# One decoder layer on one core: the expert gather and its turn become one matmul group, and the front weights come laid out by the host

## The reference

```python
proj = h @ w_in                                # front weights: w_ada (modulation), w_in, w_o
x = x + g1 * (o @ w_o)
h = rms_norm(x, norm2_g) * (1.0 + sc2) + sh2
logits = h @ router_w + router_b
top_val, top_idx = lax.top_k(logits, 4)        # 4 of 32 experts for each token
gate = softmax(top_val)
# each expert e, for the tokens that picked it:
u = x_e @ w_up[e] + b_up[e]                    # w_up[e] 1024 x 2048
glu, lin = split(u)
act = min(glu, 7) * sigmoid(1.702 * glu) * (clip(lin, -7, 7) + 1)
y_e = act @ w_down[e] + b_down[e]              # w_down[e] 1024 x 1024
y[token] += gate * y_e
```

## Time and profile before

| | |
|---|---|
| times of three runs | 1163.48, 1164.04, 1168.39 us (median 1164.04) |
| time of the profiled execution | 1164.73 us |
| span of the profiled execution | 1163.0 us |
| PE busy (matmul) | 1115.0 us, 96%, 5666 records |
| PE loads (PEld) | 498.6 us, 43% |
| DVE, ACT, POOL busy | 411.7 us, 191.1 us, 28.7 us |
| moved by DMA | 460.96 MB, mean 396 GB/s over the span |

### The profile page before, as it was taken

How to read it: one execution, slowest core, us unless ns; L and a number is a source line. 1 busy time by engine, 2 the same in 40 slices (tenths; PEclk the granted TensorE clock), 3 DMA queues, 4 the chain that set the end, 5 groups by cost and what they waited for, 6 DMA issues and landing times.

```text
span 1163.0 us, 14304 instructions
## 1 busy us (share of the span) xinstructions
PE 1115.0 (96%) x5666; PEld 498.6 (43%) x5666; DVE 411.7 (35%) x841; ACT 191.1 (16%) x385; POOL 28.7 (2%) x57
## 2 busy tenths in 40 slices
PE   7999999999999999999999998999999999999996
PEld 4777778843333333333333333333333333333332
DVE  3134653343333333333333334333333333333334
ACT  2152223321111111111111111111111111111112
POOL 0101110000000000000000000000000000000001
PEclk9999999999999999999999998999999999999998
DMA  9998996999999999999999999999999999999995
GB/s 335 377 297 227 322 349 229 371 359 392 419 419 422 427 425 429 427 429 428 429 428 428 429 427 429 427 429 426 428 428 427 429 429 429 427 429 427 428 427 212
DMA packets 52474, 460.96 MB, mean 396 GB/s; under 512 B 7156, under 2 KB 8128, under 8 KB 26152
## 3 DMA queue, kind: packets, MB, share of 16 engines
q1 hardware_dynamic: 46160, 449.66, 93.4%
q0 software_dynamic: 2752, 9.47, 3.5%
q10 hardware_dynamic: 3512, 1.14, 0.5%
HBM read 455.60 MB, written 4.65 MB: 396 GB/s over the span
## 4 chain that ended last, share of the span: by engine, by line
PE 75%; DMA 22%; SPq 1%; DVE 1%; ACT 1%; issue 0%; DVEq 0%; ACTq 0%
PE bank L1433 28%; DMA ring<-in_w_up 18%; PE bank L1488 15%; PE bank L1095 9%; PE bank L1474 5%; PE bank L1404 4%; DMA ring<-in_w_down 3%; PE bank L1316 2%; PE bank L1451 2%; PE bank L1040 1%; DMA ring<-in_w_ada 1%; PE bank L1413 1%; PE bank L1199 1%; PE bank L1462 1%; SPq L473 1%; PE bank L1176 1%
## 5 line engine op out<-in xcount | busy, mean ns | idle before, releaser
L1433 PE MATMUL bank<-ring,arena 128*64 128x512 f32 x2016 | 448.2, 595 | 21.5 <-DMA ring<-in_w_up 20.2
L1433 PEld LDWEIGHTS bank<-ring,arena 128*64 128x64 f32 x2016 | 139.8, 137 | 320.1 <-issue 277.7
L1488 PE MATMUL bank<-ring,arena 128*64 128x512 f32 x992 | 220.1, 595 | 1.3 <-DMA ring<-in_w_down 1.3
L1488 PEld LDWEIGHTS bank<-ring,arena 128*64 128x64 f32 x992 | 68.6, 137 | 131.3 <-issue 129.1
L1095 PE MATMUL bank<-arena,ring 128*128 128x264 f32 x448 | 105.4, 390 | 0.8 <-DVE arena L1695 0.8
L2043 DVE COPY arena<-bank 128x512 f32<-128x512 f32 x32 | 22.1, 692 | 199.2 <-PE bank L1433 199.2
L901 ACT ACTIVATE arena<-bank 128x512 f32<-128x512 f32 x32 | 19.1, 598 | 439.5 <-PE bank L1433 439.5
L1095 PEld LDWEIGHTS bank<-arena,ring 128*128 128x128 f32 x448 | 83.1, 190 | 17.9 <-issue 4.5
L2097 DVE TENSOR_TENSOR arena<-bank,arena 128x512 f32<-128x512 f32 x32 | 22.1, 692 | 189.1 <-PE bank L1488 189.1
L2092 DVE TENSOR_TENSOR arena<-arena,bank 128x512 f32<-128x512 f32 x128 | 79.2, 681 | 5.4 <-PE bank L1474 5.4
L1474 PE MATMUL bank<-arena,gpickT 64*128 64x512 f32 x248 | 78.7, 628 | 0.0
(11 more groups left out here) (335 smaller groups left out, 701.2 us busy)
## 6 DMA issues: line engine op xcount, KB each, us to landing
ring<-in_w_up SPq DMA_DIRECT2D x125, 2048.0 KB, 28.5
ring<-in_w_down SPq DMA_DIRECT2D x61, 2048.0 KB, 27.6
ring<-in_w_ada SPq DMA_DIRECT2D x16, 1024.0 KB, 15.6
ring<-in_w_in SPq DMA_DIRECT2D x14, 1024.0 KB, 14.7
ring<-in_w_ada SPq DMA_DIRECT2D x16, 512.0 KB, 11.9
ring<-in_w_o SPq DMA_DIRECT2D x4, 1024.0 KB, 19.0
arena<-in_w_up SPq DMA_DIRECT2D x5, 512.0 KB, 18.5
arena<-in_w_down SPq DMA_DIRECT2D x5, 512.0 KB, 12.1
```

The costliest lines, as they stand in the source:

```text
L1433: last = mm(bank[64 * half:64 * half + 64, b, :], xe[:, par, k % 4, k // 4, :], src[:, 512 * half:512 * half + 512], start=(k == 0), stop= ...
L1488: last = mm(bank[64 * half:64 * half + 64, b, :], acts[:, k, :], src[:, 512 * half:512 * half + 512], start=(k == 0), stop=(k == KT - 1))
```

## The change

Four things are changed.

1. Gather and turn are one group of matmuls. `h2tok` is now the stationary operand (128 tokens x 128 features, every second float of a row) and `pick` the moving one (64 columns). The result has the features in the partitions at once. There are 16 matmuls for an expert in place of 4 matmuls, a copy on ACT and 4 transposes. `take_gathered`, `turn`, the tile `xg` and the semaphore `gathered` are gone; DVE makes the next pick when `turned` has come.
2. ACT writes `h2tok` in four pieces of 512 floats in place of two of 1024, and the first gather begins with the first two. To this end PE's logits come ahead of the second row turn, and the samples' statistics behind the logits.
3. `w_ada`, `w_in` and `w_o` come from the host in blocks as the kernel loads them, 128 x 2048 with 8 KB of consecutive bytes for each partition. The 16 loads of half a megabyte for the first part of `w_ada` are 8 of one. A block of `w_o` now holds two column groups m for all k, so that it is used up after the second of them.
4. Expert 1 is gathered in the middle of the up matmuls of expert 0. The residual's transposes come behind these, and the residual's copies on ACT in the first turn of the loop. On DVE the first gates and the second pick come ahead of the counts for overflowing experts.

```diff
-            if kind == "out" and s == 3:
-                return "wo_psum", KT
+            if kind == "out":
+                return "wo_psum", 2 * s + 2
...
-                if kind == "ada" and c == 0:
-                    h, j = s // 4, s % 4
-                    for row in range(2):
-                        sp.dma_start(ring[:, slot, D * row:D * row + D].rearrange("p (e n) -> p e n", e=2),
...
+                src = {"ada": a["w_ada"], "in": a["w_in"]}[kind][c, s] if kind != "out" else a["w_o"][s]
+                sp.dma_start(ring[:, slot, :], src).then_inc(sem(f"slot{slot}"), 16)
...
+            def take_rows_of(i, j):
+                act.wait_ge(sem("h2tok_psum"), 2 * j + i + 1)
+                od.did(A(h2tok[:, i, 512 * j:512 * j + 512], bank[:, 4 + 2 * i + j, :], ACT.Copy, scale=rst[:, i:i + 1]),
+                       sem("h2tok_sb"))
...
-            def take_gathered(n):
-                act.wait_ge(sem("gathered"), n + 1)
-                act.activation(xg, bank[:, 6, :], ACT.Copy).then_inc(sem("xg_ready"), 1)
...
             def gather(n, first_blocks=True):
                 pe.wait_ge(sem("pick_ready"), n + 1 if first_blocks else n + 2)
-                if isinstance(n, int) and n == 0:
-                    pe.wait_ge(sem("h2tok_sb"), 2)
-                else:
+                if not (isinstance(n, int) and n == 0):
                     pe.wait_ge(sem("xe_ready"), n * XE)
-                for i in range(2):
-                    for half in range(2):
-                        last = mm(bank[64 * half:64 * half + 64, 6, :], pick[:, i, :], h2tok[:, i, 512 * half:512 * half + 512],
-                                  start=(i == 0), stop=(i == 1))
-                last.then_inc(sem("gathered"), 1)
-
-            def turn(n):
-                pe.wait_ge(sem("xg_ready"), n + 1)
-                for j in range(4):
-                    c0 = 2 * P * (j // 2) + j % 2
-                    last = tr(bank[:, 6, P * j:P * j + P], xg[:, c0:c0 + 2 * P - 1:2], ident[:, :])
+                for half in range(2):
+                    if isinstance(n, int) and n == 0:
+                        pe.wait_ge(sem("h2tok_sb"), 2 * half + 2)
+                    for j in range(4):
+                        c0 = 512 * half + 2 * P * (j // 2) + j % 2
+                        for i in range(2):
+                            last = mm(bank[:, 6, P * j + 64 * half:P * j + 64 * half + 64], h2tok[:, i, c0:c0 + 2 * P - 1:2],
+                                      pick[:, i, :], start=(i == 0), stop=(i == 1))
                 last.then_inc(sem("turned"), 1)
...
             gather(0)
             samples_routed()
-            turn(0)
             keep_going(4)
...
             up(0, 0, UP_FIRST, lo, ro, first=True)
+            gather(1)
+            up(0, UP_FIRST, UPS - 1, lo, ro)
+            up(0, UPS - 1, UPS, lo, ro)
...
             for n, n0, q in experts(pe):
-                gather(n + 1)
+                if n0 > 0:
+                    gather(n + 1)
                 back(n)
-                turn(n + 1)
```

More of the change, by code:

```diff
@@ L148, in is_plain @@
     kind, c, i = what
-    return not ((kind == "ada" and (i == 7 or (c == 0 and i == 3))) or (kind == "in" and i == 1) or (kind == "out" and i == 3))
+    return not ((kind == "ada" and (i == 7 or (c == 0 and i == 3))) or (kind == "in" and i == 1) or kind == "out")
 FRONT_USED = {}
@@ L175, in front_round @@
 def front_round(n):
-    return sum(1 + (FRONT[m][:2] == ("ada", 0)) for m in range(n + 1) if FRONT_SLOT[m] == FRONT_SLOT[n])
+    return sum(FRONT_SLOT[m] == FRONT_SLOT[n] for m in range(n + 1))
 FRONT_PLAIN = sum(_PLAIN)
@@ L921, in _, with take_residual @@
             od.did(A(gateE[:, :, :], gateE[:, :, :], ACT.Exp), sem("gate_exp"))
-            for i in range(2):
-                act.wait_ge(sem("x1tok_psum"), i + 1)
-                od.did(A(acc[i], wide(4 - 2 * i), ACT.Copy), sem("x1tok_sb"))
+            def take_residual():
+                for i in range(2):
+                    act.wait_ge(sem("x1tok_psum"), i + 1)
+                    od.did(A(acc[i], wide(4 + 2 * i), ACT.Copy), sem("x1tok_sb"))
             def take_sample_rows():
@@ L1309, in wo_part @@
             def wo_part(m, ks):
+                ld = FRONT_AT[("out", 0, m // 2)]
+                if m % 2 == 0:
+                    use_front(ld)
                 for k in ks:
-                    ld = FRONT_AT[("out", 0, k // 2)]
                     if m == 0 and k % 2 == 0:
-                        use_front(ld)
                         pe.wait_ge(sem("on_ready"), k // 2 + 1)
-                    last = mm(bank[:, WO_BANK[m % 3], 0:T], ring[:, FRONT_SLOT[ld], D * (k % 2) + P * m:D * (k % 2) + P * m + P],
+                    c0 = 2 * P * k + P * (m % 2)
+                    last = mm(bank[:, WO_BANK[m % 3], 0:T], ring[:, FRONT_SLOT[ld], c0:c0 + P],
                               oT[:, k, :], start=(k == 0), stop=(k == KT - 1))
-                    if m == KT - 1 and k % 2 == 1 and k < KT - 1:
-                        last.then_inc(sem("weights_used"), 1)
                 return last
@@ L1358, in _ @@
             row_stats(KT - 1).then_inc(sem("stat_psum"), 1)
-            turn_rows(1)
-            pe.wait_ge(sem("sq_ready"), KT + 1)
-            mm(bank[:, 2, 2 * P:2 * P + KT * TS], ones[:, :], tmpT[:, :, TP:T], start=True, stop=True)
             pe.wait_ge(sem("lt_sb"), 1)
@@ L1366, in _ @@
             last.then_inc(sem("logit_psum"), 1)
+            pe.wait_ge(sem("sq_ready"), KT + 1)
+            mm(bank[:, 3, 2 * P:2 * P + KT * TS], ones[:, :], tmpT[:, :, TP:T], start=True, stop=True
+               ).then_inc(sem("logit_psum"), 1)
+            turn_rows(1)
             for k in range(2, KT):
@@ L1585, in _ @@
             back(NE - 2)
-            turn(NE - 1)
             combine(NE - 3, SUM_BANKS, NE, NE - 2)
@@ L2228 @@
     for name in _INS:
-        x = np.ascontiguousarray(inputs[name])
+        of, lay = LAID_OUT.get(name, (name, np.asarray))
+        x = np.ascontiguousarray(lay(np.asarray(inputs[of])))
         arrays[f"in_{name}"] = x
```

102 lines of the change are left out of this document (50 added, 52 removed).

## The result

| | before | after |
|---|---|---|
| median of four runs each, on one chip | 1164.22 us | 1202.45 us (1199.36 to 1209.95) |
| ratio | | 1.0334, 95% interval 1.0307 to 1.0361: slower |
| time and span of the profiled execution | 1164.73 and 1163.0 us | 1203.83 and 1202.0 us |
| PE busy, PEld busy | 96%, 43% | 98%, 49% |
| DVE, ACT busy | 411.7, 191.1 us | 411.7, 172.0 us |

The change costs 38.2 us; the forecast was 1210 us, 46 more. The four runs after spread by 10.6 us, and this goes with the mean clock that PE was granted: 0.985 in the run of 1209.95, 0.993 in that of 1199.36. Time less (1 - clock) x span gives 1189 to 1192 for all four.

The account below looks back on a forecast made before the run. It took PE and the DMAs as close limits, with 21.5 us of PE time spare. Span: 1163.0 - 21.5 + 68.4 + 1.4 - 0.6 + 0.1 - 2.3 = 1208.5, time 1210 us; own range 1202 to 1220, 8 in 10 1190 to 1236.

Parts of the forecast that it names:

- rival A: Gather: the stride is free, 0.111 us a record, a turn grows by 1.83 us, total 1196 us; chance 0.17.
- 30 gathers in the loop: Loop, experts 2 to 31: each gather lengthens its turn by 2.28 us, +68.4 us in all.
- PE's waits for weights vanish: Loop: PE's turn becomes level with the DMAs' 29.4 us, so its 21.5 us of waits for weights go.
- start of the first gather: Ahead of expert 0: -2.3 us from the front and -0.6 from the wait for ACT's copies, -2.9 us.
- first gather to expert 0's up: First expert: gather 1.74 us becomes 4.00, the samples' spreading (0.41) and the turn (0.48) go; +1.4 us.
- expert 0's up to expert 1's: First expert: 20.66 us between the up matmuls of experts 0 and 1 becomes 20.72, +0.1 us.
- What bounds the kernel: Whole kernel: PE and DMAs lie close; PE has 21.5 us to give away, and work beyond lengthens the kernel one to one.
- The gather: Loop: 32 records at 0.125 us, 4.00 us instead of 2.25, 0.53 for the change of width moved ahead; turn +2.28 us.
- The turn: Loop: the four removed transposes (0.48 us) save nothing, since `combine`'s fourth matmul waits for DVE anyway.
- rival B: Loop: the removed turn pays after all if `combine`'s fourth matmul is freed earlier, 14.5 us less, 1196 us; chance 0.07.
- The front: Front weights: loading in one 8 KB piece per partition removes about PE's wait for `w_ada`; -2.3 us, between 0 and -4.5.
- The marks that I named: New profile: loads near 260 ns, turns of 29.4 us, hardly any weight waits, DMA share below 1, longer DVE hold, `w_ada` wait below 1 us.

Follow-up runs that it names:

- Experiment 7: The kernel before with six more matmuls on constants in each turn of the loop, behind `combine`; 1181.36 us, ratio 1.0148.
- experiment 8: The changed kernel, but ACT writes the token rows with even and odd features apart, so that the gather's stationary operand is contiguous; 1195.35 us, ratio 1.0250.
- experiment 5: The kernel before with one edit: DVE takes the next expert's tokens ahead of the first bias; 1163.55 us, ratio 0.9992.
- experiment 4: The changed kernel, but DVE takes the next expert's tokens ahead of the bias; 1169.99 us, ratio 1.0052.
- experiment 1: The kernel before with the merged gather alone, everything else left as it was; 1204.11 us, ratio 1.0346.
- experiment 6: The kernel before with three more matmuls on constants in each turn of the loop, behind `combine`; 1166.28 us, ratio 1.0011.
- experiment 2: The changed kernel with the old gather and turn put back, all other edits kept; 1164.32 us, ratio 1.0004.
- experiment 9: The changed kernel with four constant matmuls of 512 columns, two ahead of the wait for the ranks and two ahead of the first gather; 1202.57 us, ratio 1.0329.
- experiment 10: The changed kernel with tokens taken ahead of the bias, contiguous token rows, and one constant matmul at each of two places before the first gather; 1168.62 us, ratio 1.0048.
- experiment 3: The kernel before with the host's layout of the front weights and the new `w_o` blocks alone; 1166.25 us, ratio 1.0016.

## Why the prediction was nearly right, and where it was not

The sum was +45.5 us of span, and +39.0 were measured. That the two are so near is in part luck: the gather's term was 7.5 us too high and the returned waits 5.2 too small, and the clock's fall, which the forecast didn't have, adds 4.9 against them. Without it the kernel would stand near 1198 us, below the forecast's own range (1202 to 1220) and at rival A's 1196. Its terms, with what the two traces show. "Start" is that of the first piece of chain named.

| term | predicted | measured | from |
|---|---|---|---|
| 30 gathers in the loop | +68.4 | +60.9 | turns of 29.08 and 27.05 us (means 29.17 and 27.14) |
| PE's waits for weights vanish | -21.5 | -26.7 | what is left of the sum once the other rows are taken, see below |
| start of the first gather | -2.9 | -1.4 | 236.88 to 235.50 |
| first gather to expert 0's up | +1.4 | +1.1 | 5.81 us at full clock against 4.70 |
| clock at the first gather | 0 | +4.9 | 9.77 - 5.81, and 7.96 - 7.02 in the first half of up |
| expert 0's up to expert 1's | +0.1 | +0.2 | 267.02 - 245.27 - 0.94 against 20.59 |

**What bounds the kernel: right, and it decided.** The loss follows the turn only beyond PE's spare time. Its size was a fifth too small. The list of waits shows 21.5 us, but a turn at the DMAs' pace takes 29.36 against 27.05 undisturbed, 2.3 us more. Its two waits in the timeline of PE before are only 0.52 and 1.24:

```profile
955.95 3.65 PE L1433 MATMUL bank<-ring,arena 128*64 128x512 f32 x16 [0.52 <-DMA ring<-in_w_up]
960.85 3.65 PE L1433 MATMUL bank<-ring,arena 128*64 128x512 f32 x16 [1.24 <-DMA ring<-in_w_up]
```

About 0.5 us of each such turn is lost and isn't in the list. 23 waits are about 12 such turns, so about 6 us more, near enough to the difference between 21.5 and 26.7. From expert 1's up to expert 29's, 28 turns, the traces give 796.2 and 832.6 us: 28 x 2.03 = 56.8, of which 20.4 came back, where the list has 16.5 us of waits for weights in that stretch; the two last turns and the tail give the other 6.3. Experiment 7 says the same from the other side: 26.8 us are free.

**The gather: the mechanism was right, the size of one term too high.** It was forecast at 0.125 us a record by the strided transposes (1.12 x 0.111), and is 0.118: in these loads the stride makes it 1.06 times. The load lasts 196 ns and not 260; the 67 ns were read from transposes (208 against 141), and don't add to a load of a float32 matmul, which takes 192 ns contiguous. That is 32 x 0.007 = 0.2 us a turn, 7 us in all, and the largest error of the sum. Rival A (free) said 0.111, as far from 0.118 as the forecast's 0.125; experiment 8, where the operand is contiguous, shows 0.1115 and costs 7 us less in the medians, 10 by the ratios. A's 1196 us is 6.5 from the measured median and the forecast's 1210 is 7.5, so A stands at least as near. The change of width went ahead of the gather, as forecast: the new gather's first load has 0.81 us of idle ahead of it and `back` now begins without one.

That the load and not the 64 moving columns sets the pace was not tried by an edit, but two neighbouring lines of the kernel before bear it out. Both move 32 columns; L1389 loads 8 columns and L1391 loads 128. In the chain 16 records of the one take as long as 4 of the other:

```profile
239.03 0.56 PE bank L1389 x16
239.59 0.56 PE bank L1391 x4
```

The rule in the Trainium skill ("SBUF — State Buffer", section "Door 1: The DMA port swizzle"), by which every second float32 is free, holds for neither: 6% here, 12% in the transposes. The 81 ns that the Trainium skill gives in "TensorE: Matmul & The Clock Gate", section "Back-to-back issue gap", were not reached by loads of 128 columns in the rows here: 0.1115 us apart in the contiguous gather, 0.106 in transposes. By that figure the change would have cost next to nothing.

**The turn: right, for a reason read only half.** I booked nothing for the four transposes because DVE holds the fourth matmul of `combine`, and the hold grew from 0.50 us (2.42 - 1.92, experiment 5) to 0.98, by just the 0.48 that the transposes had taken. What I had not worked out from the earlier trace rows is how long this hold already was before, and that one moved call removes all of it. That made my expectation for experiment 4 wrong by half. It also says what the forecast's rival B needed: not an earlier DVE, but another order on it.

**The front: the lead was there and was not kept.** I booked -2.3 of 0 to -4.5. PE's first long projection piece starts at 38.45 instead of 42.72, 4.3 us earlier, near the far end of the range: the matmuls at 24 to 30 us ran at the full clock (1.00), where the kernel before had 0.50. But the profile before starts this piece later than any other of the old layout: experiments 1, 5, 6 and 7 have 40.83 to 41.41. All seven profiles of the new layout have 37.54 to 38.77, so the lead is about 3 us, and the 2.3 that I booked is not far off. The wait itself I had put in the wrong place: its 2.25 us end at 23.99, where the DMAs give 384 GB/s, not in the stretch of 362. The lead is still 4.3 us when POOL issues the store of the samples' values, at 139.70 against 143.96. Then the chain after goes through this store and the broadcast back, which POOL issues too:

```profile
139.70 5.57 DMA sample_values<-ring
145.55 2.06 POOL arena L636 x3
147.61 17.01 DMA arena<-sample_values
164.91 1.92 DVE ring L1821 x7
```

and DVE waits for it. The timeline of DVE at this place in the kernel before:

```profile
160.07 2.19 DVE L1839 SCALAR_TENSOR_TENSOR ring<-arena,ring 128x128 f32<-128x128 f32 x8 [4.07 <-DMA arena<-sample_values]
165.02 2.19 DVE L1839 SCALAR_TENSOR_TENSOR ring<-arena,ring 128x128 f32<-128x128 f32 x8 [0.77 <-DMA arena<-sample_values]
```

And the same instructions in the kernel after:

```profile
158.26 2.19 DVE L1821 SCALAR_TENSOR_TENSOR ring<-arena,ring 128x128 f32<-128x128 f32 x8 [6.53 <-DMA arena<-sample_values]
164.64 2.19 DVE L1821 SCALAR_TENSOR_TENSOR ring<-arena,ring 128x128 f32<-128x128 f32 x8 [2.22 <-DMA arena<-sample_values]
```

The store was issued 4.3 us earlier; the first values landed 1.8 us earlier (158.26 against 160.07) and the last 0.4 earlier (164.64 against 165.02). I had written that faster front loads elsewhere meet a PE that never waited for them; the wait that they did meet was DVE's, one step behind. In the new layout's other profiles the last of it lands at 164.50 to 166.37, no earlier than with the old one (162.72 to 165.73 where DVE waits for it). Why isn't shown; it shares the DMA engines with the weights that fill the ring in that time, and I didn't try it without them.

That wait has a second price that I had overlooked. PE in turn waits for DVE: 2.2 to 3.3 us between 158 and 170 us with the new layout, 0.2 to 1.7 with the old. Its granted clock falls there in six of the seven profiles of the new layout (0.60 to 0.93 between 160 and 170 us, the changed kernel's own is the exception) and in none of the five of the old one. In experiment 2, with 0.93 and 0.73 in these ten us, one group of 16 records in the chain takes 5.25 us, where the same group takes 3.56 in the kernel before, at 166.31:

```profile
164.38 5.25 PE bank L1097 x16
```

So the 1.4 us by which the first gather starts earlier in the table is no more than the spread: without constant matmuls ahead of it, it starts at 234.99 to 236.88 with the old layout and at 235.50 to 237.66 with the new one. Experiment 2 shows that whatever is left is worth nothing as long as the DMAs set the end.

**The clock: not foreseen.** At the first gather the granted clock falls to 0.50, back at 1.00 some 10 us later, and this costs 4.9 us. Ahead of it PE ran matmuls of mostly 32 to 128 moving columns with gaps between them (busy 4.61 of 5 us from 230 to 235), then the gather's 32 loads with 64 columns moving. The same 32 loads in the loop, between matmuls of 512 columns, don't lower it (1.00 at 900 to 1000). In experiments 9 and 10, with constant matmuls ahead of the gather, the clock stays up. It does so in experiment 8 without them too, so that the constants did it is likely and not shown. The old gather at this place is not safe from it either: the clock is 1.00 from 235 to 240 in the profile before, in experiments 2, 3 and 7, and 0.66 in experiments 5 and 6, where the first gather takes 3.3 and 3.5 us and not 1.94; but by 240 it is full again. So what the merged form adds in these profiles is the length of the fall, not the fall. The 4.9 us are taken from the times at either level in two kernels, not from one edit alone.

**The marks that I named.** Turns of 29.1 (29.4 forecast), no weight waits, no wait for `w_ada` and the longer hold came as forecast. Wrong were the loads' 260 ns (196) and the DMA share below 1: with 29.08 us a turn against 29.4 it is 1.00.

## What to carry to other kernels

Fewer steps are not less work. Here the choice of the stationary operand decided what the float32 matmuls cost: with 64 columns moving, the records come at the pace of their 128-column loads, 0.11 to 0.12 us, so 16 such matmuls take 3.91 us, more than twice the 1.72 of 4 with 512 columns moving. Before counting a removed instruction, look for the wait behind it, and read how long that wait is already: here it swallowed the removed turn whole, and moving one call on DVE was worth about 30 us in one kernel and nothing in the other, because there another resource set the end.

## What the hardware showed that I had not expected

- A stationary operand that takes every second float costs 0.118 us a record in float32 matmuls against 0.1115 contiguous, while in transposes the load itself goes from 141 to 208 ns.
- The granted clock is 0.50 from 240 to 245 us while PE is busy all 5 us of it, in all three profiles that have the strided gather and no constant matmuls ahead of it (the changed kernel, experiments 1 and 4). In experiments 8 and 10, with contiguous rows, and in experiment 9, with constant matmuls, it is 1.00.
- A wait costs PE more than the idle time in front of the waiting matmul: about 0.5 us more in a turn with two waits of 0.52 and 1.24 us.
- In the front, waits of PE of 2.2 to 3.3 us come with a granted clock of 0.60 to 0.93 between 160 and 170 us in six of seven profiles of the new layout, so part of a lead is paid back behind the wait.
